# Seven operand blocks with a signal each, a new order of GpSimd's work, and the first rows of the second half beside the last jobs of the first

## The chip, the cores and the metric

One NeuronCore of a Trainium2 chip. The metric is the time of one execution on the device, in microseconds (us). The engines are TensorE (PE; PEld is its weight load), VectorE (DVE), ScalarE (ACT), GpSimd (POOL) and SyncE (SP, which only issues DMAs here). SBUF is the on-chip memory, PSUM the banks that TensorE writes.

## What is computed

A trunk layer over 2048 latent tokens of width 1024 and 256 context tokens. What matters here is its beginning:

```python
h = rmsnorm(x, norm_w) * (1.0 + scale[:, None]) + shift[:, None]
hc = rmsnorm(ctx, norm_w) * (1.0 + scale_c) + shift_c
cols = in_projection(h, w_in, ALL_IN_NAMES)           # h @ w_in, 1024 -> 9 x 1024 + 32
cols_c = in_projection(hc, w_in, ("m_xbc", "m_dt"))
```

Some columns then pass a convolution of width 3 over the tokens (m_xbc with a SiLU behind it, h_proj without), some a SiLU or a sigmoid. The state-space mixer, the long convolutions and the merge come later and are not touched.

## The kernel before

**Products.** The product h @ w_in is made in fp32 quality from parts that TensorE reads fast: each operand is split into a high part (a rounded copy, by ScalarE) and a low part (operand minus high part), and each product is high x high + high x low + low x high: three matmuls. Besides, a pair of weight tiles (128 output channels each) times four blocks of the operand goes with seven block products instead of eight, by sums of blocks on both sides.

**Operand (class Operands).** The tokens go in two halves of 1024. A round k (of KQ = 4) loads two tiles of rows (`load`), multiplies them by the norm (`scale`, DVE) and adds the shift (`shift`, ScalarE), makes T1, T3, T2, N4 (`sums`, GpSimd), then high parts (`high`, ScalarE) and low parts (`low`, DVE) of all seven blocks B11, B21, B22, T1, T2, T3, N4. Before, they went in three groups with a signal each: B11, then B21 with B22, then the four sums in one instruction of 2048 columns. The first half is made in `phase_norm`, beside the projection of the context; the second in `phase_in_projection`, before job NJ. It overwrites the same hi and lo tiles.

**Jobs (phase_in_projection).** A job J is a pair of weight tiles over one half of the tokens, seven products j = 0 to 6 of 12 matmuls each (4 rounds by 3). There are NJ = 37 jobs per half, 74 in all, one of each half with a single tile (J = 8, 45). Jobs 0 to 7 are conv_silu (the first six turned: their rows are also transposed on TensorE and stored by token), 9 to 20 conv, 21 to 36 silu or sigmoid; the second half repeats them from 37 on. Products need the blocks of the weights in the order A11, A12, S2, S3, S1, A22, S4, those of the operand in the order B11, B21, T2, T3, T1, N4, B22.

**The order around a job, written out by hand.** While TensorE makes the products of job J:
- ScalarE, per product j: waits for it, copies product 0 to r1 (L808), makes the high part of block j of job J+1 (`split`, L743; that of S2, S3, S1, S4 waits for its sum), then at j = 3 and 5 `finish` for job J-1 (SiLU or copy, and a store); for turned jobs, at j = 2 and 4, three DMA issues (L773 to L775; two, L777 and L778, in the second half).
- GpSimd: the four sums of the weight tiles of job J+1 (L666 to L671), then its seven low parts (L678).
- DVE: adds each product to the result (`take`, L843 to L859), and between them the convolution of job J-1 (L872 to L885) and the copies of turned rows (L895).
- TensorE: from product 4 on also transposes of job J-1 (L697), behind the signal of `finish`.
- SP: loads weight tiles into three buffers, a tile when the one three before it has been split. The loads for the second half stand in job NJ+1's place.
At job NJ each engine runs all four rounds of the operand, and TensorE waits before each round of each product (L714: the signal of the block's group). raw (two buffers) takes the results of a job and, at the switch, the loaded rows; the sums of the operand lay in res.

## Time and profile before

| | us |
|---|---|
| median of 3 runs | 3819.22 (3813.38 to 3819.71) |
| profiled execution | 3822.45 |
| its span, first to last instruction | 3820.7 |
| TensorE busy | 3432.2 (90%) |
| DVE busy | 2280.6 (60%) |
| GpSimd busy | 1865.3 (49%) |
| ScalarE busy | 1523.4 (40%) |
| mean granted clock of TensorE | 0.950 |

Times of rows are counted from the first instruction. In a group of instructions, the number behind the bar is the busy time, then the mean of one in ns, then the idle time before them and what ended it.

### The profile page before, as it was taken

How to read it: one execution, taken by the hardware profiler on the slowest of the kernel's cores; microseconds unless marked ns; L12 is line 12 of the kernel's file. 1: busy time of each engine (PE TensorE's matmuls, PEld its weight loads, DVE VectorE, ACT ScalarE, POOL GpSimd, SP SyncE). 2: the span in 40 equal slices, each digit the busy share in tenths (PEclk: the TensorE clock that was granted, in tenths of full speed). 3: DMA queues.
4: the chain of work that ended last, by engine and by line, in shares of the span. 5: the costliest groups of instructions: out<-in, count | busy, mean ns of one | idle time of the engine just before them, and what ended most of it. 6: DMA issues, size and time to landing. Idle time of an engine off the chain costs nothing. (4 is left out here: it accounts for less than half of the span.)

```text
span 3820.7 us, 45518 instructions
## 1 busy us (share of the span) xinstructions
PE 3432.2 (90%) x16246; PEld 2839.7 (74%) x16246; DVE 2280.6 (60%) x2870; ACT 1523.4 (40%) x2933; POOL 1865.3 (49%) x1146
## 2 busy tenths in 40 slices
PE   6799999995999999966998999999667886999998
PEld 2677888884888888844996887887546776788886
DVE  5686885224878852236543676666386666577662
ACT  3423223334332233322775554554245553333332
POOL 0477998775879987721000101101167562545442
PEclk8899999997999999988999999999698998999999
DMA  7444333333333333358997847865494445556562
GB/s 260 153 135 142 118 112 107 111 111 109 122 127 116 111 111 111 110 216 330 284 297 197 186 125 166 191 154 120 156 381 157 145 153 167 189 191 212 183 199 99
DMA packets 406346, 636.42 MB, mean 167 GB/s; under 512 B 154731, under 2 KB 241691, under 8 KB 403091
## 3 DMA queue, kind: packets, MB, share of 16 engines
q1 hardware_dynamic: 305661, 442.22, 37.8%
q10 hardware_dynamic: 91256, 157.83, 11.3%
q0 software_dynamic: 9216, 33.56, 3.9%
q8 instruction: 130, 2.13, 0.2%
q14 instruction: 83, 0.68, 0.1%
HBM read 430.49 MB, written 203.03 MB: 166 GB/s over the span
## 5 line engine op out<-in xcount | busy, mean ns | idle before, releaser
L715 PE MATMUL pl_bank<-hl_hi,pl_a_hi 128*128 128x512 f32 x2056 | 811.1, 394 | 67.5 <-DVE hl_lo L354 45.7
L717 PE MATMUL pl_bank<-hl_hi,pl_a_lo 128*128 128x512 f32 x2056 | 803.6, 391 | 0.0
L716 PE MATMUL pl_bank<-hl_lo,pl_a_hi 128*128 128x512 f32 x2056 | 803.0, 391 | 0.0
L715 PEld LDWEIGHTS pl_bank<-hl_hi,pl_a_hi 128*128 128x128 f32 x2056 | 388.0, 189 | 150.5 <-DVE hl_lo L354 37.9
L678 POOL TENSOR_TENSOR pl_a_lo<-pl_sums,pl_a_hi 128x512 fp32r<-128x512 f32 x288 | 433.4, 1516 | 130.1 <-ACT pl_a_hi L743 130.1
L717 PEld LDWEIGHTS pl_bank<-hl_hi,pl_a_lo 128*128 128x128 f32 x2056 | 387.7, 189 | 82.0
L716 PEld LDWEIGHTS pl_bank<-hl_lo,pl_a_hi 128*128 128x128 f32 x2056 | 388.3, 189 | 78.2
L743 ACT ACTIVATE pl_a_hi<-pl_sums 128x512 fp32r<-128x512 f32 x288 | 181.9, 633 | 511.7 <-PE pl_bank L717 468.7
L2018 POOL TENSOR_TENSOR mo_w_lo<-mo_w,mo_w_hi 128x1024 fp32r<-128x1024 f32 x96 | 238.8, 2491 | 276.0 <-ACT mo_w_hi L2089 276.0
L678 POOL TENSOR_TENSOR pl_a_lo<-pl_w,pl_a_hi 128x512 fp32r<-128x512 f32 x220 | 307.7, 1413 | 101.5 <-ACT pl_a_hi L743 101.2
L2046 PE MATMUL mo_bank<-mo_hi,mo_w_hi 128*128 128x512 f32 x768 | 305.9, 398 | 21.4 <-POOL mo_w_lo L2018 17.1
L885 DVE SCALAR_TENSOR_TENSOR pl_res<-pl_raw,pl_taps,pl_res 128x1023 f32<-128x1023 f32 (+1 forms) x160 | 309.4, 1934 | 3.0
L2047 PE MATMUL mo_bank<-mo_lo,mo_w_hi 128*128 128x512 f32 x768 | 300.6, 391 | 0.0
L2048 PE MATMUL mo_bank<-mo_hi,mo_w_lo 128*128 128x512 f32 x768 | 300.4, 391 | 0.0
L1393 DVE TENSOR_TENSOR conv_prod<-conv_bank,conv_spec 128x512 f32<-128x512 f32 x256 | 173.8, 690 | 158.5 <-PE conv_bank L1286 113.3
L743 ACT ACTIVATE pl_a_hi<-pl_w 128x512 fp32r<-128x512 f32 x220 | 137.9, 629 | 290.4 <-PE pl_bank L717 282.5
L1346 ACT COPY conv_v<-conv_bank 128x256 f32<-128x256 f32 x256 | 154.2, 602 | 223.3 <-PE conv_bank L1297 223.3
L1205 POOL DMA_DIRECT2D conv_gin<-u_s x32 | 36.8, 1152 | 382.8 <-DVE conv_x L1358 382.8
L1198 POOL DMA_DIRECT2D conv_x<-u_s x16 | 18.6, 1165 | 385.5 <-POOLq L67 265.9
L2046 PEld LDWEIGHTS mo_bank<-mo_hi,mo_w_hi 128*128 128x128 f32 x768 | 145.0, 189 | 56.8 <-issue 18.4
L1111 DVE COPY spec_y<-spec_bank 64x256 f32<-64x256 f32 x256 | 109.5, 428 | 120.6 <-PE spec_bank L1085 118.6
L843 DVE TENSOR_TENSOR pl_raw<-pl_bank,pl_r 128x512 f32<-128x512 f32 x72 | 49.8, 692 | 207.8 <-PE pl_bank L717 181.6
(247 smaller groups left out, 7093.1 us busy)
## 6 DMA issues: line engine op xcount, KB each, us to landing
pl_w<-in_w_rec SPq DMA_DIRECT2D x146, 512.0 KB, 3.6
conv_spec<-spec_s SPq DMA_DIRECT2D x248, 256.0 KB, 6.1
mo_w<-in_w_br SPq DMA_DIRECT2D x96, 512.0 KB, 3.6
kern_s<-taps_res SPq DMA_DIRECT2D x16, 2048.0 KB, 7.0
spec_xin<-kern_s SPq DMA_DIRECT2D x64, 512.0 KB, 5.4
spec_s<-spec_res ACTq DMA_DIRECT2D x128, 256.0 KB, 4.0
st_xb<-tok_s SPq DMA_DIRECT2D x36, 768.0 KB, 6.4
g_s<-pl_res ACTq DMA_DIRECT2D x32, 512.0 KB, 3.0
```

The costliest lines, as they stand in the source:

```text
L678: nc.gpsimd.tensor_tensor(a_lo[:, n % NS, :], s, a_hi[:, n % NS, :].bitcast(F32), ALU.subtract).then_inc(s_lo, 1)
L715: pe.matmul(out, a_hi[:, q, m], op_hi[:, b, k, :], start=(i == 0 and k == 0), stop=False)
L716: pe.matmul(out, a_hi[:, q, m], op_lo[:, b, k, :], start=False, stop=False)
L717: mm = pe.matmul(out, a_lo[:, q, m], op_hi[:, b, k, :], start=False, stop=(i == len(terms) - 1 and k == KQ - 1))
L743: nc.scalar.activation(a_hi[:, n % NS, :], src, ACT.Copy).then_inc(s_hi, 1)
L885: nc.vector.scalar_tensor_tensor(out=dst, in0=src[:, i:i + width], scalar=taps[i], in1=dst, op0=ALU.mult, op1=ALU.add).then_inc(s_conv, 1)
L1346: nc.scalar.copy(v[:, :, k], bank[2 + k % 2][:, 0:CB]).then_inc(s_vm, 1)
L1393: nc.vector.tensor_tensor(prod[:, n % 4], bank[ubank[k % 4]][:, None, 0:CB].to_broadcast([P, 2, CB]), spec[:, n // 2 % SLOT, :, k % 2], AL ...
L2018: nc.gpsimd.tensor_tensor(w_lo[:, s % 3, :], w[:, s % 3, :], w_hi[:, s % 3, :].bitcast(F32), ALU.subtract).then_inc(s_wlo, 1)
L2046: pe.matmul(bank[s % 4][:], w_hi[:, q, m], hi[:, slot, k, :], start=(k == 0), stop=False)
L2047: pe.matmul(bank[s % 4][:], w_hi[:, q, m], lo[:, slot, k, :], start=False, stop=False)
L2048: mm = pe.matmul(bank[s % 4][:], w_lo[:, q, m], hi[:, slot, k, :], start=False, stop=(k == KT - 1))
```

## The change

- The seven blocks of a round get a signal each, in the order of use (ORDER); `high` and `low` make one block of 512 columns at a time. In `phase_norm` they are spread over three steps. `sums` waits for each block to be free, not for all.
- At the switch the sums of the operand lie in tok, the buffer of turned rows, and no longer in res.
- Round 0 of the second half moves beside job 36 (NJ-1): `scale` after product 3, `shift` after 4, high parts after 5 and 6 and the last two at the head of job 37, before the finishes of job 36; GpSimd's sums of round 0 stand between the low parts of S3 and S1 of job 37. Rounds 1 to 3 stay at the head of job 37. SP waits for DVE's last add of job 36 besides.
- GpSimd makes the low parts of A11 and A12 of a job before the four sums, the other five after them; it waits for the second weight tile only before the sums. The first tile of a pair is given free after the low part of A22.
- The finishes of silu, sigmoid and single jobs move from products 3 and 5 to 0 and 1.

```diff
@@ -289,8 +289,10 @@
     B11, B21, B22, T1, T2, T3, N4 = range(7)
-    GROUP = (0, 1, 1, 2, 2, 2, 2)
-    PARTS = 3
+    ORDER = (B11, B21, T2, T3, T1, N4, B22)
+    PLACE = {b: i for i, b in enumerate(ORDER)}
+    SUM = {T1: 1, T3: 2, T2: 3, N4: 4}
+    PARTS = 7
...
@@ -321,36 +323,50 @@
     def sums(self, pool, k):
...
-        t1, t2, t3, n4 = (self.tmp[:, i // 2, i % 2] for i in range(4))
+        t1, t2, t3, n4 = (self.tmp(b) for b in (self.T1, self.T2, self.T3, self.N4))
+
+        def free(b):
+            if k:
+                pool.wait_ge(self.s_lo, self.PARTS * (k - 1) + self.PLACE[b] + 1)
+
         pool.wait_ge(self.s_norm, 2 * k + 2)
         if k:
-            pool.wait_ge(self.s_lo, self.PARTS * k)
+            pool.wait_ge(self.s_sum, 4 * k)
+        free(self.T1)
         self.nc.gpsimd.tensor_tensor(t1, b12, b11, ALU.subtract).then_inc(self.s_sum, 1)
+        free(self.T3)
         self.nc.gpsimd.tensor_tensor(t3, b22, b12, ALU.subtract).then_inc(self.s_sum, 1)
+        free(self.T2)
         pool.wait_ge(self.s_sum, 4 * k + 1)
         self.nc.gpsimd.tensor_tensor(t2, b22, t1, ALU.subtract).then_inc(self.s_sum, 1)
+        free(self.N4)
         pool.wait_ge(self.s_sum, 4 * k + 3)
         self.nc.gpsimd.tensor_tensor(n4, b21, t2, ALU.subtract).then_inc(self.s_sum, 1)
...
+    def high(self, act, k, i):
+        op, src, hi, lo = self.part(k, i)
+        if op in self.SUM:
+            act.wait_ge(self.s_sum, 4 * k + self.SUM[op])
+        else:
+            act.wait_ge(self.s_norm, 2 * k + (1 if op == self.B11 else 2))
         self.nc.scalar.activation(hi, src, ACT.Copy).then_inc(self.s_hi, 1)
 
-    def low(self, dve, k, g):
-        src, hi, lo = self.part(k, g)
-        dve.wait_ge(self.s_hi, self.PARTS * k + g + 1)
+    def low(self, dve, k, i):
+        op, src, hi, lo = self.part(k, i)
+        dve.wait_ge(self.s_hi, self.PARTS * k + i + 1)
         self.nc.vector.tensor_tensor(lo, src, hi.bitcast(F32), ALU.subtract).then_inc(self.s_lo, 1)
...
@@ -454,11 +470,8 @@
                     k = n // 4
                     if n % 4 == 0:
                         ops.shift(act, k)
-                    elif n % 4 == 1:
-                        ops.high(act, k, 0)
-                        ops.high(act, k, 1)
-                    elif n % 4 == 2:
-                        ops.high(act, k, 2)
+                    for i in ((), (0, 1), (2, 3, 4), (5, 6))[n % 4]:
+                        ops.high(act, k, i)
...
@@ -496,14 +509,15 @@
             for n in range(2 * KT):
                 k = n // 4
                 if n % 4 == 0:
+                    for i in (5, 6) if k else ():
+                        ops.low(dve, k - 1, i)
                     ops.scale(dve, k)
...
+                for i in ((), (), (0, 1), (2, 3, 4))[n % 4]:
+                    ops.low(dve, k, i)
...
+            for i in (5, 6):
+                ops.low(dve, KQ - 1, i)
             conv(2 * KT - 1)
@@ -562,7 +576,7 @@
                 freed[p0[J] + j] = ("act", ea0[J] + 1) if j == 0 else ("dve", ed0[J] + (0, 1, 2, 3, 5, 6, 7)[j])
         w_done[w0[J]] = a0[J] + 2
         if prods is PAIR:
-            w_done[w0[J] + 1] = a0[J] + 6
+            w_done[w0[J]] = w_done[w0[J] + 1] = a0[J] + 6
...
@@ -587,7 +601,7 @@
         s_turn, s_tev, s_tst = ph.sem("turn"), ph.sem("turn_out"), ph.sems("tst", 2)
         ops = Operands(nc, ph, t, keep, rows[:].rearrange("p a n -> p (a n)"), 1, op_hi, op_lo,
                        lambda q, r: raw[:, (NJ + q) % 2, r, 0:HW],
-                       res[:, 0:2, 0:HW].rearrange("p a (b n) -> p a b n", b=2))
+                       lambda b: tok[:].rearrange("p a c n -> p (a c n)")[:, (b - B.T1) * QW:(b - B.T1 + 1) * QW])
@@ -639,6 +653,7 @@
                     sp.wait_ge(s_fin, fin0[NJ - 1])
                     ops.load(sp, 0)
                     sp.wait_ge(s_fin, fin0[NJ])
+                    sp.wait_ge(s_ed, ed0[NJ])
                     for k in range(1, KQ):
                         ops.load(sp, k)
@@ -657,30 +672,42 @@
         def _(pool):
             for J, job in enumerate(jobs):
                 wt = [w[:, (w0[J] + i) % NW, :] for i in range(len(job.tiles))]
-                for i in range(len(job.tiles)):
-                    pool.wait_ge(s_w[(w0[J] + i) % NW], 16 * ((w0[J] + i) // NW + 1))
+                pool.wait_ge(s_w[w0[J] % NW], 16 * (w0[J] // NW + 1))
                 if J:
                     pool.wait_ge(s_lo, a0[J])
+                half = [[tl[:, 0:QW], tl[:, QW:D]] for tl in wt]
+                n = 4 * pairs[J]
+
+                def total(i, x, y, op):
+                    nc.gpsimd.tensor_tensor(sums[:, i], x, y, op).then_inc(s_sum, 1)
+
+                def low(i, src):
+                    at = a0[J] + i
+                    pool.wait_ge(s_hi, at + 1)
+                    nc.gpsimd.tensor_tensor(a_lo[:, at % NS, :], src, a_hi[:, at % NS, :].bitcast(F32), ALU.subtract
+                                            ).then_inc(s_lo, 1)
+
+                low(A11, half[0][0])
+                low(A12, half[0][1])
                 if len(job.tiles) == 2:
-                    n = 4 * pairs[J]
-                    nc.gpsimd.tensor_tensor(sums[:, 0], wt[1][:, 0:QW], wt[1][:, QW:D], ALU.add).then_inc(s_sum, 1)
+                    pool.wait_ge(s_w[(w0[J] + 1) % NW], 16 * ((w0[J] + 1) // NW + 1))
+                    total(0, half[1][0], half[1][1], ALU.add)
                     pool.wait_ge(s_sum, n + 1)
-                    nc.gpsimd.tensor_tensor(sums[:, 1], sums[:, 0], wt[0][:, 0:QW], ALU.subtract).then_inc(s_sum, 1)
-                    nc.gpsimd.tensor_tensor(sums[:, 2], wt[0][:, 0:QW], wt[1][:, 0:QW], ALU.subtract).then_inc(s_sum, 1)
+                    total(1, sums[:, 0], half[0][0], ALU.subtract)
+                    total(2, half[0][0], half[1][0], ALU.subtract)
                     pool.wait_ge(s_sum, n + 2)
-                    nc.gpsimd.tensor_tensor(sums[:, 3], wt[0][:, QW:D], sums[:, 1], ALU.subtract).then_inc(s_sum, 1)
-                    src = (wt[0][:, 0:QW], wt[0][:, QW:D], sums[:, 1], sums[:, 2], sums[:, 0], wt[1][:, QW:D], sums[:, 3])
-                else:
-                    src = (wt[0][:, 0:QW], wt[0][:, QW:D])
-                for i, s in enumerate(src):
-                    n = a0[J] + i
-                    pool.wait_ge(s_hi, n + 1)
-                    nc.gpsimd.tensor_tensor(a_lo[:, n % NS, :], s, a_hi[:, n % NS, :].bitcast(F32), ALU.subtract
-                                            ).then_inc(s_lo, 1)
+                    total(3, half[0][1], sums[:, 1], ALU.subtract)
+                    low(S2, sums[:, 1])
+                    low(S3, sums[:, 2])
+                    if J == NJ:
+                        for q in range(2):
+                            pool.wait_ge(s_tst[q], 16 * stores_before(t0[NJ] + q))
+                        ops.sums(pool, 0)
+                    low(S1, sums[:, 0])
+                    low(A22, half[1][1])
+                    low(S4, sums[:, 3])
                 if J == NJ:
-                    for q in range(3):
-                        pool.wait_ge(s_st[q], 16 * ((f0[NJ] + 2 - q) // 3))
-                    for k in range(KQ):
+                    for k in range(1, KQ):
                         ops.sums(pool, k)
@@ -710,7 +737,7 @@
                         q = (a0[J] + a) % NS
                         for k in range(KQ):
                             if J == NJ:
-                                pe.wait_ge(ops.s_lo, B.PARTS * k + B.GROUP[b] + 1)
+                                pe.wait_ge(ops.s_lo, B.PARTS * k + B.PLACE[b] + 1)
...
@@ -782,16 +809,19 @@
             for J, prods in enumerate(products):
                 nxt = a0[J + 2] - a0[J + 1] if J + 1 < 2 * NJ else 0
                 if J == NJ:
+                    act.wait_ge(s_mm, p0[NJ])
+                    ops.high(act, 0, 5)
+                    ops.high(act, 0, 6)
                     for m in order(J - 1):
                         finish(J - 1, m)
-                    act.wait_ge(s_mm, p0[NJ])
-                    ops.shift(act, 0)
-                    for k in range(KQ):
+                    ops.shift(act, 1)
+                    for k in range(1, KQ):
                         ops.high(act, k, 0)
                         ops.high(act, k, 1)
                         if k + 1 < KQ:
                             ops.shift(act, k + 1)
-                        ops.high(act, k, 2)
+                        for i in range(2, B.PARTS):
+                            ops.high(act, k, i)
                 for j in range(max(len(prods), nxt, 7)):
                     if j < len(prods):
                         n = p0[J] + j
@@ -808,10 +838,15 @@
                             nc.scalar.activation(r1[:], bank[n % 4][:], ACT.Copy).then_inc(s_ea, 1)
                     if j < nxt:
                         split(J + 1, j)
-                    if J and J != NJ and j in (3, 5):
-                        m = (j == 3) * 1
-                        if m in order(J - 1):
-                            finish(J - 1, m)
+                    if J and J != NJ:
+                        for m in order(J - 1):
+                            if j == (5 - 2 * m if jobs[J - 1].conv is not None else 1 - m):
+                                finish(J - 1, m)
+                    if J == NJ - 1:
+                        if j == 4:
+                            ops.shift(act, 0)
+                        for i in {5: (0, 1, 2, 3), 6: (4,)}.get(j, ()):
+                            ops.high(act, 0, i)
                     if j == 2 and J >= 2 and jobs[J - 2].turned:
@@ -905,20 +940,27 @@
             when = {0: ((1, 0), (1, 1)), 1: ((1, 2),), 2: ((0, 0),), 3: ((0, 1), (0, 2))}
             for J, prods in enumerate(products):
                 if J == NJ:
-                    dve.wait_ge(s_mm, p0[NJ])
-                    ops.scale(dve, 0)
-                    for k in range(KQ):
+                    for i in (4, 5, 6):
+                        ops.low(dve, 0, i)
+                    ops.scale(dve, 1)
+                    for k in range(1, KQ):
                         ops.low(dve, k, 0)
                         ops.low(dve, k, 1)
                         if k + 1 < KQ:
                             ops.scale(dve, k + 1)
-                        ops.low(dve, k, 2)
+                        for i in range(2, B.PARTS):
+                            ops.low(dve, k, i)
                 for j in range(7):
                     if prods is PAIR:
                         take(J, j)
                     if J and jobs[J - 1].conv is not None:
                         for m, op in when.get(j, ()):
                             conv(J - 1, m, op)
+                    if J == NJ - 1:
+                        if j == 3:
+                            ops.scale(dve, 0)
+                        for i in (0, 1, 2, 3) if j == 6 else ():
+                            ops.low(dve, 0, i)
                     if j < len(prods) and turn_at(J, j):
                         turned_out(*turn_at(J, j))
```

## Rows read from the trace of the kernel before

**Rows 1.** Page, costliest groups: one of TensorE's three of the in-projection
```profile
L715 PE MATMUL pl_bank<-hl_hi,pl_a_hi 128*128 128x512 f32 x2056 | 811.1, 394 | 67.5 <-DVE hl_lo L354 45.7
```
**Rows 2.** Waits of PE, 160 to 1665 us: total us, times, longest
```profile
PE pl_bank L715 <- DVE hl_lo L354: 45.7, 5, 11.9
...
PE pl_turned L697 <- ACT pl_res L753: 6.4, 6, 2.2
```
**Rows 3.** Timeline (start, length, what, [idle before]), a conv job: ACT, POOL
```profile
500.65 0.60 ACT L808 ACTIVATE pl_r<-pl_bank 128x512 f32<-128x512 f32 x1 [2.00 <-PE pl_bank L717]
...
519.69 0.60 ACT L808 ACTIVATE pl_r<-pl_bank 128x512 f32<-128x512 f32 x1 [2.01 <-PE pl_bank L717]
...
517.76 1.30 POOL L678 TENSOR_TENSOR pl_a_lo<-pl_sums,pl_a_hi 128x512 fp32r<-128x512 f32 x1 [0.40 <-ACT pl_a_hi L743]
```
**Rows 4.** Timeline, start of the in-projection: ACT, POOL, PE
```profile
165.47 1.15 ACT L743 ACTIVATE pl_a_hi<-pl_w 128x512 fp32r<-128x512 f32 x2 [7.88 <-DMA pl_w<-in_w_rec]
...
171.88 2.49 POOL L678 TENSOR_TENSOR pl_a_lo<-pl_w,pl_a_hi 128x512 fp32r<-128x512 f32 x2
...
173.29 0.77 PE L715 MATMUL pl_bank<-hl_hi,pl_a_hi 128*128 128x512 f32 x1 [21.78 <-POOL pl_a_lo L678]
```
**Rows 5.** Timeline, DVE: a long and a short low part of the operand
```profile
119.77 2.28 DVE L354 TENSOR_TENSOR hl_lo<-nl_tmp,hl_hi 128x2048 fp32r<-128x2048 f32 x1
...
907.31 0.69 DVE L354 TENSOR_TENSOR hl_lo<-pl_raw,hl_hi 128x512 fp32r<-128x512 f32 x1 [1.73 <-ACT hl_hi L349]
```
**Rows 6.** Timeline, ACT: r1 copies of jobs 36 and 38
```profile
881.45 0.60 ACT L808 ACTIVATE pl_r<-pl_bank 128x512 f32<-128x512 f32 x1 [2.01 <-PE pl_bank L717]
...
971.43 0.60 ACT L808 ACTIVATE pl_r<-pl_bank 128x512 f32<-128x512 f32 x1 [2.01 <-PE pl_bank L717]
```
**Rows 7.** The switch: timeline of ACT and DVE; DMA issues (KB, median us to landing)
```profile
900.07 1.06 ACT L763 ACTIVATE pl_res<-pl_raw 128x1024 f32<-128x1024 f32 x1 [0.46 <-ACT pl_res L763]
...
903.10 2.47 DVE L311 SCALAR_TENSOR_TENSOR pl_raw<-pl_raw,keep_mod,rt_rows 128x1024 f32<-128x1024 f32 x2 [4.64 <-DMA pl_raw<-in_xT]
...
924.11 2.47 DVE L311 SCALAR_TENSOR_TENSOR pl_raw<-pl_raw,keep_mod,rt_rows 128x1024 f32<-128x1024 f32 x2 [2.61 <-DMA pl_raw<-in_xT]
...
pl_raw<-in_xT SPq DMA_DIRECT2D x8, 512.0 KB, 5.2
```
**Rows 8.** Job 4: timeline of ACT, DVE, PE; L885's ns min/median/max
```profile
268.72 0.63 ACT L743 ACTIVATE pl_a_hi<-pl_w 128x512 fp32r<-128x512 f32 x1 [2.15 <-PE pl_bank L717]
271.93 0.64 ACT L743 ACTIVATE pl_a_hi<-pl_sums 128x512 fp32r<-128x512 f32 x1 [2.58 <-PE pl_bank L717]
...
277.11 1.04 ACT L753 ACTIVATE pl_res<-pl_res 128x1023 f32<-128x1023 f32 x1
...
269.25 2.09 DVE L885 SCALAR_TENSOR_TENSOR pl_res<-pl_raw,pl_taps,pl_res 128x1023 f32<-128x1023 f32 x1
...
278.20 0.66 PE L697 MATMUL pl_turned<-pl_ident,pl_res 128*128 128x128 f32 x4 [0.70 <-ACT pl_res L753]
...
L885 DVE SCALAR_TENSOR_TENSOR pl_res<-pl_raw,pl_taps,pl_res x160: 1275/2194/2332, 196.0 to 1371.7; 128x1023 f32<-128x1023 f32 x80, 128x1025 f32<-128x1025 f32 x80
```
**Rows 9.** Job 2: ACT, PE; stretches (us, busy of each engine, PEclk, DMA, GB/s)
```profile
225.05 4.73 ACTq L775 DMA_DIRECT2D tok_s<-pl_tok  x1
...
231.53 1.08 PE L697 MATMUL pl_turned<-pl_ident,pl_res 128*128 128x128 f32 x4 [2.15 <-ACT pl_res L753]
...
232.84 0.63 PE L716 MATMUL pl_bank<-hl_lo,pl_a_hi 128*128 128x512 f32 x1
...
232.00:234.00 2.00, 2.00 (x7) 1.71 (x7) 0.00 (x0) 0.61 (x1) 1.28 (x1) 0.50 0.83 293
...
910.00:920.00 10.00, 0.67 (x2) 0.57 (x3) 5.58 (x5) 5.67 (x5) 5.51 (x5) 0.50 0.02 4
```
**Rows 10.** Timeline, ACT: job 41
```profile
1037.94 0.64 ACT L743 ACTIVATE pl_a_hi<-pl_w 128x512 fp32r<-128x512 f32 x1 [2.16 <-PE pl_bank L717]
...
1044.01 0.64 ACT L743 ACTIVATE pl_a_hi<-pl_sums 128x512 fp32r<-128x512 f32 x1 [2.23 <-PE pl_bank L717]
```

30 lines of the change are left out of this document (12 added, 18 removed).

## Prediction

> **What bounds the kernel now.** I read the page first: TensorE is busy for 90% of the span, and its three largest groups (one of them is [rows 1]), some 800 us each, are the in-projection. So only what stops TensorE there counts. The view of its waits over that stage lists 45.7 us in five waits for DVE's low parts of the operand and 6.4 us in six waits for ScalarE's finished rows [rows 2]; a third, of 21.8 us for GpSimd's low part of the weights, is the start [rows 4]. In a plain job the engine is full: from one r1 copy to the next is 19.04 us, seven products of 2.72 [rows 3]. Shorter work on another engine gains nothing there, and a later step costs nothing until its slack is used up. What the two stalls at the starts can give back is known; the question is what the new order of GpSimd and ScalarE does to the jobs between them.
>
> **1. First job of the in-projection.** GpSimd now makes the low part of A11 before the four sums. Before, the high part of A11 was ready at 166.05 (165.47 and half of the 1.15 us for two), the low part came out at 173.1, and TensorE began at 173.29 [rows 4]. Now the low part takes 1.25 us from 166.1, so TensorE begins at 167.5: 5.8 us earlier. The third product needs low S2, behind low A12 and four sums: seven operations of 1.25 to 1.27 from 166.1 end near 175.0, while two products (4.55 and 2.72, the first at the low clock) end at 174.8. It gives back 0.4. **-5.4 us** (-4 to -6).
>
> **2. Context stage (phase_norm).** DVE's groups follow each other without idle time there, so DVE sets the pace. Three low subtractions per pair of rows become seven of 512 columns. One of 2048 took 2.28 us, one of 512 0.69 [rows 5]. Four short ones for a long one cost between nothing (the extra time is overlap at their ends) and 4 x 0.69 - 2.28 = 0.48; I take 0.25 in each of four rounds: **+1.0 us** (0 to 2; the four sums beside them contend as before).
>
> **3. The switch to the second half.** The r1 copies before and after lie at 881.45 and 971.43, 90.0 us for two jobs that need 38.1 [rows 6]: 51.9 us is the most that could go. The clock is at its lower level (0.50) in this stretch [rows 9]. Today the first rows are scaled at 903.10, behind the finishes of job 35, and each later round ends with the low parts of the sums, then a load (5.2 us to landing, its pair 0.2 to 0.4 behind: 5.4), for which DVE waits before it scales, as at 924.11 [rows 7].
> The change moves round 0 beside the last pair of jobs. Job 35's two finishes move to the first two products of job 36, so rows 0 are asked for at 885.9 (881.45, and the r1, A11 and A12 copies and the finish that now follow) and land near 892, beside two stores. Scaling (2.5) and shifting (1.2 more) end at 895.7, the four sums at 901. But the next rows overwrite the buffer of job 36 and so wait for both of its finishes, and these now stand behind all seven high parts of round 0 on ScalarE: B22's ends at 902.9, the finishes (1.06 and 0.46 before it, each) at 905.5 where the second ended at 901.1. So the load of round 1 is 4.4 us later than now. It lands at 912; scale and shift to 915.6; the two low parts beside GpSimd to 919.4; scale 2 and its shift to 923; five high parts and the last low parts, two of them beside GpSimd, to 927.5; load of round 3 to 933; scale and shift to 936.5; five high parts and B11 to 939.7; low B11 of round 3 near 941.7. From there TensorE never waits again, since each block has its own signal: the end of product 0 at the low clock (1.3), product 1 partly so (3.8), five of 2.72: 960.5. Today that job ends at 968.5. **-8.0 us** (-3 if one more low part is held up in each round, -14 if the loads land in 4.5 us and no low part is). So 44 of the 51.9 us stay.
> The rule "2.0 us + bytes / 436 GB/s" of the Trainium skill (DMA: Bandwidth & Descriptors, "Anatomy of one DMA") makes 4.4 us of a pair of loads, where the rows show 5.4; with two on the chain the whole sum would be 2 us less by it. I go by the rows.
>
> **4. Turned jobs, first half (2 to 6).** This is where the change takes back. ScalarE's copy of S2 waits for sums 0 and 1. Before, GpSimd had them done while ScalarE waited for TensorE; now they stand behind low A12, which waits for A12's high part, which waits for product 1. In job 4 [rows 8]: A12's copy ends at 269.35. DVE's scalar_tensor_tensor gets the port at 269.25 and, alone, takes 1.28: GpSimd waits to 270.5 (today it is DVE that waits there: 2.09 us). Low A12 to 271.8, sum 0 to 273.0, sum 1 to 274.3. S2's copy starts there instead of 271.93: 2.4 us later (1.4 with no contention; 3.1 if the next DVE operation gets in too). Behind it on ScalarE stand the three DMA issues of the turned rows (some 4.5 us whatever the start: the third one alone took 4.73 in job 2, where no store of turned rows was under way before [rows 9]), S3's copy, the SiLU at 277.11, and for that SiLU TensorE waits already: its transposes start at 278.20, just after it ends at 278.15. So all of the delay reaches TensorE, and so every job of the five gets longer: 5 x 2.4 = 12.1 us. Job 1 has no such issues; its S3 copy comes 1.8 later, of which 0.9 shows.
> The port rule of the Trainium skill (SBUF — State Buffer, "SBUF: two separate sides") says that whoever starts first holds the shared pair for the whole instruction. By it each held GpSimd operation takes its full 1.29 after the release; the rows give about 1.15. The copy would be 0.1 later per job, 0.7 us in the sum.
> **The clock.** In job 2 TensorE stood still for 2.15 us before the transposes, and the granted clock fell to 0.50 between 232 and 235; matmuls took 0.63 instead of 0.39 us and about 1.3 us was lost [rows 9]. In the other jobs it idles less (0.70 in job 4, 4.2 us over five of them by [rows 2]) and the clock stays. With 2.4 more, jobs 3 to 6 idle 3.1 to 3.5, longer than what let it fall. I add 4 x 1.3 = 5.2. Sum of part 4: **+18.2 us** (+8 with 1.4 and no fall, +25 with 3.1 and falls in all six).
>
> **5. Turned jobs, second half (38 to 43).** Fewer descriptors, so no long issue, and TensorE does not wait today. S3's copy now waits for sum 2: A12's copy ends at 1038.58, low A12 at 1040.9, sum 1 at 1043.5, DVE's tensor_scalar 0.55, sum 2 at 1045.2; the copy starts there instead of at 1044.01 [rows 10]. The SiLU ends at 1046.9, product 4 ended near 1046.5: 0.4 us in each of five jobs. In job 38, the first SiLU after the sigmoids, a table load stands between S3's copy and the SiLU, and TensorE waits for it already; it comes 1.95 us later in full, and the wait grows to some 2.8 us, so I add 1.3 for the clock. **+5.2 us** (+1 to +9).
>
> **6. The plain and conv jobs, moved finishes, loads.** GpSimd is busy 18.5 of 19.04 us in a conv job (its longest wait there is 0.40) [rows 3], and the new order makes it idle 1.8 us before A11 and 1 before A12. It does not become the bound: DVE's operations now run in these gaps instead of against it, and S4's low part ends about 1 us later than now, while low A11 cannot start before the high one anyway. Its product is 14 us away, S2's 7. The second weight tile is now loaded after low A22, not low A12, and so some 10 us later; it lands about 4 us before sum 0 wants it. SP's queue has the context loads behind it, which are needed a job later. The finishes of silu and sigmoid jobs move from products 3 and 5 to 0 and 1, where ScalarE waits 1.7 us for TensorE. Nothing.
>
> **Sum.** -5.4 + 1.0 - 8.0 + 18.2 + 5.2 = +11.0 us. The profiled execution took 3822.45 us (3820.7 of span and 1.75 around it), so 3833.4 by it; it lies 3.2 above the median 3819.22, so I say **3830.2**.
>
> **Rivals.**
> A, the forecast: 3830, by its own bounds 3827 to 3838. Chance 0.50.
> B, the same mechanism, small: the clock does not fall and the copy is 2 us late: 11.0 - 6.5 - 2 = +2.5, 3822. For it: idle of 1 us left the clock alone. 0.22.
> C, the switch gives its upper bound, -14: +5, 3824. 0.08.
> D, faster. The third DMA issue ends when the queue has drained, at a time of its own, and not a fixed time after its start; then S3's copy and the SiLU come as today and part 4 is 0.9. With the switch at -10: -5.4 + 1 - 10 + 0.9 + 5.2 = -8.3, 3811. It decides once the SiLU of jobs 2 to 6 is under 0.8 us late. Against it: the issue is longest in job 2, with an empty queue. 0.10.
> E, GpSimd becomes the bound in the 28 conv jobs: if DVE's operations don't fit the gaps, each job leaves it 0.6 us later, and after some ten the slack of S2 is gone; another 12 us, 3842. 0.10.
> Under 0.2% (7.6 us) a measurement of this kernel tells little from no change. Slower by more: A nearly whole, E: 0.59. Same: B, C, the lower edge of A: 0.31. Faster: 0.10. The range reaches from below B and C, 3814 (part 4 at its lower bound of 8 with the rest as forecast gives 3820, the switch at -14 with it 3814), to E, 3841.
>
> **What would show it.** In the trace after: TensorE's first in-projection matmul some 5 us after the first weight lands; S2's copy in jobs 2 to 6 about 9 us after the r1 copy (6.5 now) and r1 copies over 25 us apart (22.7 now); clock 0.50 once in each; r1 copies 82 us apart across the switch, the load of round 1 near 905; low parts of plain jobs on time. It would be wrong if the copy of S2 were late and the SiLU not, or if r1 copies of conv jobs were over 19.04 apart.

## The result, and the profile of the changed kernel

| | before | changed |
|---|---|---|
| median of 10 runs each, us | 3818.99 | 3839.24 |
| lowest to highest | 3813.38 to 3821.63 | 3826.02 to 3845.56 |
| profiled execution, us (its span) | 3822.45 (3820.7) | 3835.30 (3833.5) |
| mean granted clock in it | 0.950 | 0.951 |

The ratio of the medians' runs is 1.005, 95% interval 1.0041 to 1.0059: slower by about 19 us, or 20 by the medians. One execution of all those told of below took 5129 us, at a mean granted clock of 0.644; no ratio includes it. The forecast was 3830.2, with 3841 as its upper end. The direction is right, the size is 9 us short, and the way there is right only in part.

Page and waits of the changed kernel, as in [rows 1] and [rows 2] (same stretch, 160 to 1665 us; L742 is the old L715, L724 the old L697, L770 the old L743, L687 the old L678):

```profile
L742 PE MATMUL pl_bank<-hl_hi,pl_a_hi 128*128 128x512 f32 x2056 | 813.1, 395 | 64.3 <-DVE hl_lo L370 41.8
...
PE pl_bank L742 <- DVE hl_lo L370: 41.8, 4, 16.6
PE pl_bank L742 <- POOL pl_a_lo L687: 22.5, 4, 15.4
PE pl_turned L724 <- ACT pl_res L780: 18.5, 12, 4.6
```

The operand's wait fell by only 4 us, and that for finished rows grew from 6.4 to 18.5. Inside the 22.5 us for GpSimd are two waits of 3.3 in the middle of the stage that were not there before. The start, as [rows 4] (columns: start, length, engine, line, what, [idle before it <- released by]):

```profile
165.33 1.15 ACT L770 ACTIVATE pl_a_hi<-pl_w 128x512 fp32r<-128x512 f32 x2 [7.98 <-DMA pl_w<-in_w_rec]
...
166.10 2.49 POOL L687 TENSOR_TENSOR pl_a_lo<-pl_w,pl_a_hi 128x512 fp32r<-128x512 f32 x2 [17.47 <-ACT pl_a_hi L770]
...
167.51 0.76 PE L742 MATMUL pl_bank<-hl_hi,pl_a_hi 128*128 128x512 f32 x1 [15.44 <-POOL pl_a_lo L687]
```

TensorE begins at 167.51 where it began at 173.29. To see where this goes, I took the first matmul of every job from PE's timeline in both traces, and call the time to the next job's first matmul the job's length:

| job | before | changed | difference | forecast |
|---|---|---|---|---|
| start of job 0 | 173.29 | 167.51 | -5.8 | -5.8, and +1.0 for the context stage |
| 0 | 20.87 | 21.22 | +0.4 | +0.4 |
| 1 | 20.14 | 26.91 | +6.8 | +0.9 |
| 2, 3, 4 | 25.43, 22.70, 22.36 | 23.65, 23.70, 23.24 | -1.8, +1.0, +0.9 | +2.4, +3.7, +3.7 |
| 5, 6 | 22.72, 22.73 | 23.45, 25.75 | +0.7, +3.0 | +3.7, +3.7 |
| 9 and 46 (each follows the single-tile job) | 19.28, 19.29 | 24.44, 24.43 | +5.2, +5.1 | 0 |
| 36 and 37 (switch) | 89.98 | 84.74 | -5.2 | -8.0 |
| 38 | 20.68 | 24.10 | +3.4 | +3.25 |
| 39 to 43, each | 21.2 | 21.8 | +0.56 | +0.4 |
| plain and conv jobs | 19.04 | 19.04 | 0 | 0 |

The sum is +16.5 us at the start of the last job. The spans differ by 12.8: stages in which nothing was changed took 3.7 less in this one execution, and in the medians the difference is 20.

**Job 4**, as [rows 8]:

```profile
269.32 0.63 ACT L770 ACTIVATE pl_a_hi<-pl_w 128x512 fp32r<-128x512 f32 x1 [2.15 <-PE pl_bank L744]
274.97 0.63 ACT L770 ACTIVATE pl_a_hi<-pl_sums 128x512 fp32r<-128x512 f32 x1 [5.01 <-POOL pl_sums L682]
...
276.16 1.75 ACTq L802 DMA_DIRECT2D tok_s<-pl_tok  x1
278.03 0.63 ACT L770 ACTIVATE pl_a_hi<-pl_sums 128x512 fp32r<-128x512 f32 x1 [2.43 <-issue]
278.57 1.04 ACT L780 ACTIVATE pl_res<-pl_res 128x1023 f32<-128x1023 f32 x1
...
279.66 0.65 PE L724 MATMUL pl_turned<-pl_ident,pl_res 128*128 128x128 f32 x4 [1.56 <-ACT pl_res L780]
```

S2's copy comes 5.65 us after A12's where it was 3.2: 2.4 late, as worked out, and GpSimd's sums are named. But the third store issue behind it takes 1.75 us where it took 3.57, and the SiLU is only 0.9 late against the r1 copy. In jobs 3, 5 and 6 it is 1.0, 0.7 and 1.4 late, in job 2 not at all.

**Job 9**, which no step of the prediction looked at:

```profile
370.10 0.62 ACT L770 ACTIVATE pl_a_hi<-pl_w 128x512 fp32r<-128x512 f32 x1
...
370.80 1.28 POOL L687 TENSOR_TENSOR pl_a_lo<-pl_w,pl_a_hi 128x512 fp32r<-128x512 f32 x1 [5.82 <-ACT pl_a_hi L770]
372.04 1.28 POOL L682 TENSOR_TENSOR pl_sums<-pl_w 128x512 f32<-128x512 f32 x1
...
374.72 0.63 ACT L770 ACTIVATE pl_a_hi<-pl_sums 128x512 fp32r<-128x512 f32 x1 [4.00 <-POOL pl_sums L682]
...
378.51 0.71 PE L742 MATMUL pl_bank<-hl_hi,pl_a_hi 128*128 128x512 f32 x1 [3.29 <-POOL pl_a_lo L687]
```

The single-tile job has two long products (5.44 and 8.16 us). A12's high part waits for the second, so its low part waits too, and GpSimd stands idle for 5.82 us with the four sums behind that wait. Job 9's third product needs low S2, and TensorE stands 3.3 us for it. The kernel before has the same wait of 5.82 us, but it had made the sums ahead of both low parts (job 8 starts at 350.61 there, job 9 at 364.21):

```profile
343.99 2.29 POOL L671 TENSOR_TENSOR pl_sums<-pl_w,pl_sums 128x512 f32<-128x512 f32 x1
357.49 2.29 POOL L678 TENSOR_TENSOR pl_a_lo<-pl_w,pl_a_hi 128x512 fp32r<-128x512 f32 x1 [11.21 <-ACT pl_a_hi L743]
365.60 1.30 POOL L678 TENSOR_TENSOR pl_a_lo<-pl_w,pl_a_hi 128x512 fp32r<-128x512 f32 x1 [5.82 <-ACT pl_a_hi L743]
```

**Job 1**, and the clock (in the last three lines: stretch and its length; busy time of PE, PEld, DVE, ACT, POOL; granted clock; DMA's busy share and GB/s):

```profile
207.11 1.12 PE L724 MATMUL pl_turned<-pl_ident,pl_res 128*128 128x128 f32 x4 [4.61 <-ACT pl_res L780]
...
205.00:207.00 2.00, 0.00 (x0) 0.00 (x0) 0.46 (x1) 1.52 (x2) 2.00 (x3) 0.50 0.00 0
232.00:234.00 2.00, 1.26 (x8) 1.13 (x9) 1.73 (x3) 1.32 (x2) 2.00 (x2) 1.00 0.53 162
...
379.00:381.00 2.00, 2.00 (x6) 1.59 (x5) 0.00 (x0) 1.54 (x3) 2.00 (x3) 0.50 0.37 149
```

After job 9's stall the granted clock is at its lower level, 0.50 (1.2 GHz), as it was in job 2 before [rows 9]; in job 2 of the changed kernel it is 1.00. Outside the switch it fell in jobs 1, 6, 9, 38 and 46, each time in or just behind a pause of 2.3 us or more.

### The profile page after: what moved, and what is told of

The parts are those of the page before. It is cut to its first block and busy times, and to the rows that moved or that the text cites. A ratio compares the mean times of both kernels' runs of the same rounds, so it can differ in the third digit from the quotient of the medians.

```text
span 3833.5 us, 45593 instructions
## 1 busy us (share of the span) xinstructions
PE 3439.1 (90%) x16246; PEld 2840.7 (74%) x16246; DVE 2268.1 (59%) x2902; ACT 1525.3 (40%) x2965; POOL 1846.5 (48%) x1146
## 5 line engine op out<-in xcount | busy, mean ns | idle before, releaser
L742 PE MATMUL pl_bank<-hl_hi,pl_a_hi 128*128 128x512 f32 x2056 | 813.1, 395 | 64.3 <-DVE hl_lo L370 41.8
L743 PE MATMUL pl_bank<-hl_lo,pl_a_hi 128*128 128x512 f32 x2056 | 804.9, 391 | 0.0
L742 PEld LDWEIGHTS pl_bank<-hl_hi,pl_a_hi 128*128 128x128 f32 x2056 | 389.1, 189 | 148.4 <-DVE hl_lo L370 41.4
L687 POOL TENSOR_TENSOR pl_a_lo<-pl_w,pl_a_hi 128x512 fp32r<-128x512 f32 x220 | 339.3, 1544 | 243.3 <-ACT pl_a_hi L770 241.9
L743 PEld LDWEIGHTS pl_bank<-hl_lo,pl_a_hi 128*128 128x128 f32 x2056 | 389.3, 189 | 78.8
L687 POOL TENSOR_TENSOR pl_a_lo<-pl_sums,pl_a_hi 128x512 fp32r<-128x512 f32 x288 | 412.5, 1453 | 54.5 <-ACT pl_a_hi L770 54.5
L770 ACT ACTIVATE pl_a_hi<-pl_sums 128x512 fp32r<-128x512 f32 x288 | 181.7, 633 | 569.1 <-POOL pl_sums L682 372.3
L2088 PE MATMUL mo_bank<-mo_hi,mo_w_hi 128*128 128x512 f32 x768 | 306.0, 398 | 23.3 <-POOL mo_w_lo L2060 17.1
L920 DVE SCALAR_TENSOR_TENSOR pl_res<-pl_raw,pl_taps,pl_res 128x1023 f32<-128x1023 f32 (+1 forms) x160 | 277.8, 1736 | 3.0
L770 ACT ACTIVATE pl_a_hi<-pl_w 128x512 fp32r<-128x512 f32 x220 | 137.9, 629 | 253.8 <-PE pl_bank L744 225.2
L682 POOL TENSOR_TENSOR pl_sums<-pl_w 128x512 f32<-128x512 f32 x144 | 203.7, 1414 | 0.7 <-DMA pl_w<-in_w_rec 0.6
```

What stands on the lines that cost most here:

```text
L682: nc.gpsimd.tensor_tensor(sums[:, i], x, y, op).then_inc(s_sum, 1)
L687: nc.gpsimd.tensor_tensor(a_lo[:, at % NS, :], src, a_hi[:, at % NS, :].bitcast(F32), ALU.subtract).then_inc(s_lo, 1)
L742: pe.matmul(out, a_hi[:, q, m], op_hi[:, b, k, :], start=(i == 0 and k == 0), stop=False)
L743: pe.matmul(out, a_hi[:, q, m], op_lo[:, b, k, :], start=False, stop=False)
L770: nc.scalar.activation(a_hi[:, n % NS, :], src, ACT.Copy).then_inc(s_hi, 1)
L920: nc.vector.scalar_tensor_tensor(out=dst, in0=src[:, i:i + width], scalar=taps[i], in1=dst, op0=ALU.mult, op1=ALU.add).then_inc(s_conv, 1)
```

## The experiments

All ran beside the kernel before; its median in these comparisons was 3816 to 3819 us.

### Two ends: the order of the sums alone, and all but it

The first is the kernel before, with only this changed: GpSimd's order (told in words here) and, since the sums need it, the later release of the first tile (`w_done` counts the low parts after which a tile is given free):

```
-                totals 0 to 3; low A11, A12, S2, S3, S1, A22, S4
+                low A11, A12; totals 0 to 3; low S2, S3, S1, A22, S4
-        w_done[w0[J]] = a0[J] + 2
+        w_done[w0[J]] = a0[J] + 6
```

> The kernel before, with GpSimd's new order and the later release of the first weight tile alone; nothing of the switch, the seven blocks or the finishes is changed. Theory 1 (order of the sums): TensorE starts 5 us earlier, job 1 takes 26.9 us, jobs 9 and 46 take 24.4, job 38 some 24, jobs 39 to 43 some 21.8; the switch is as before. From the differences of the two traces 3819 + 21 = 3840 us. Theory 3 (moved finishes): jobs 9 and 46 stay at 19.3 and the time is near 3830. The prediction's own terms give 3819 + 18 = 3837, with job 1 at 21 and jobs 2 to 6 at 26.

3835.1 us, ratio 1.004 (1.0026 to 1.0053). Jobs 9 and 46 take 24.3 and 24.4 us, job 1 24.9, jobs 2 to 6 23.5, 25.5, 23.2, 24.8 and 23.9; the switch is as before (89.5). The second is the changed kernel with the old order, and the old release of the first tile, back from job 1 on (in short):

```
+                ahead = J == 0 or len(job.tiles) == 1
+                if ahead: low(A11), low(A12)
                 total 0 to 3
+                if not ahead: low(A11), low(A12)
                 low(S2) ...
```

> The changed kernel, with GpSimd's old order (four sums, then low A11 and A12) and the old release of the first weight tile in every job but the first. The first job keeps the new order; the seven blocks, the rows of round 0 beside the last pair, and the moved finishes stay. Theory 1 (the sums standing behind low A12 make the stalls): jobs 9 and 46 fall from 24.4 us to 19.3, jobs 2 to 6 go back to 22.4 to 25.4, jobs 39 to 43 to 21.2, job 38 to 20.7; the switch keeps its -5. Of the 5.8 us that the first job gives, most is lost in job 1 anyhow, since GpSimd works without a pause from 166 us to the end of job 1 in both kernels and ends there only 0.8 us earlier: about 3813 us. Theory 2 (the prediction's: the gain of the start stays): 3808. Theory 3 (the moved finishes or the later loads make the stalls of jobs 9 and 46): these stay at 24.4 if it is the finishes, about 3823.

3809.4 us, ratio 0.9977 (0.9966 to 0.9987), which is faster than the kernel before by 0.2%. Jobs 9 and 46 are back at 19.3, jobs 2 to 6 at 23.8, 22.7, 22.3, 22.6 and 22.7, jobs 39 to 43 at 21.2. Beside job 9's start ScalarE now finds the sums made, and takes two without a wait:

```profile
361.43 1.14 ACT L777 ACTIVATE pl_a_hi<-pl_sums 128x512 fp32r<-128x512 f32 x2
...
361.61 1.30 POOL L689 TENSOR_TENSOR pl_a_lo<-pl_w,pl_a_hi 128x512 fp32r<-128x512 f32 x1 [5.82 <-ACT pl_a_hi L777]
362.87 3.80 POOL L689 TENSOR_TENSOR pl_a_lo<-pl_sums,pl_a_hi 128x512 fp32r<-128x512 f32 x3
```

GpSimd still waits 5.82 us, with nothing behind it that is wanted. So the order costs what the change loses, and the moved finishes, which both this kernel and the changed one have, are not the cause in jobs 9 and 46.

### Which low part does it

The changed kernel with low A11, the sums, then low A12, from job 1 on, and the old release of the first tile there.

> The changed kernel, with GpSimd's order low A11, four sums, low A12 from the second job on, and the old release of the first weight tile. Theory 1 in its narrow form: only low A12 in front of the sums hurts, since its high part waits for the second product of the job before; low A11 needs only the r1 copy. Then S2's copy starts 9.5 us after the job's first matmul as before, jobs 9 and 46 take 19.3 us, and the time is that of the run with the sums first, about 3813, give or take 2. In its wide form (any low part in front of the sums hurts): S2's copy is about 1 us late, job 9 and 46 some 1 us, jobs 2 to 6 some 0.5 us each, 3818.

3813.5 us, ratio 0.9988 (0.9979 to 0.9997). Jobs 9 and 46 take 19.3, jobs 39 to 43 21.2: low A12 in front of the sums is what hurts there. In jobs 1 and 2 to 6 it is not wholly free: 25.9; 25.4, 22.7, 23.3, 22.6, 25.7, with clock falls in jobs 1, 2 and 6. The profiled execution took 3826.7 us, the longest of its 11, so these lengths may be on the high side; the kernel before has 25.4 in job 2 as well. What of the rest is the order's is open.

### The later load

The changed kernel, where the first tile of a pair is released after low S2 (`a0[J] + 3`) instead of low A22.

> The changed kernel with one thing undone in half: the first weight tile of a pair is given back after low S2, the first low part that comes after all four sums, and no longer after low A22. Theory 1 (the later loads play no part): all jobs as in the changed kernel, job 1 at 26 to 27 us, jobs 9 and 46 at 24.4, the time within 3 us of it (3839). Theory 4 (the second weight tile lands late and holds the sums): job 1 is 2 us or more shorter, and sum 0 of job 2 starts before 198 us.

3837.3 us; job 1 27.1, jobs 9 and 46 24.4, sum 0 of job 2 at 199.34 us (199.23 in the changed kernel). In the changed kernel the later load of the first tile's buffer plays no part.

### What the first job's early start is worth

The same kernel as the second above, with the old order in job 0 too.

> The run with the sums first, but in the first job too, so that nothing of GpSimd's order is new; the seven blocks, round 0 beside the last pair, and the moved finishes stay. Against the run with the sums first in all jobs but the first (3809) it prices the new order of the first job alone. Theory 1 (GpSimd is the chain from the first weights to the end of job 1, so that most of the earlier start is given back): TensorE starts 5.8 us later, jobs 0 and 1 together are 3 to 4.5 us shorter, 1.5 to 2 us in all: 3811. Prediction's theory (0.4 given back): 5 us, 3814. The switch should be 85 us for its two jobs in both.

3813.0 us, ratio 0.9981 (0.9972 to 0.9990), so all of the change but GpSimd's order is worth some 7 us (4 to 11 by the interval). TensorE starts at 173.63; jobs 0 and 1 take 20.8 and 20.1, where the kernel with the early start needs 22.0 and 22.9 after 167.28. Of 6.3 us, 3.9 are given back (1.2 in job 0, 2.7 in job 1) and 2.4 stay, about as expected. The medians can't tell: they differ by 3.6, the ratios to the kernel before by 0.0004, which is 1.5 us. GpSimd shows one reason. In the kernel before it works from 166.87 to 193.7 us without a pause of over 0.25, and has a little slack from there; in the changed one it works from 166.10 to 210.3 with one pause of 0.5. TensorE began 5.8 us earlier, its supplier 0.8.

In the kernel with the sums first there is a second reason, which no run takes apart from the first. Before the first sum of job 1 GpSimd stands still for a weight tile (issued at 178.48, landed at 181.74), whose buffer the first job gives free only after low A22:

```profile
182.25 1.28 POOL L684 TENSOR_TENSOR pl_sums<-pl_w 128x512 f32<-128x512 f32 x1 [2.55 <-DMA pl_w<-in_w_rec]
```

Without that wait the sum would start at 179.7, 12.4 us behind TensorE's first matmul and not 15.0. That is an estimate; in the next kernel it starts 12.2 behind, and there job 1 takes 20.3. So most of what job 1 gives back here may be the load's. In the changed kernel, where two low parts stand ahead of the sums, the tile landed at 182.59, just before the sum at 182.93, and the earlier release above gained nothing.

### Taking GpSimd off that chain

On the kernel with the sums first and stores issued earlier (next section), DVE makes the seven low parts of job 0, and GpSimd only its sums; the first tile is given free after the last of them:

```
+            for i in (A11, A12, S2, S3, S1, A22, S4):      # DVE, before its first job
+                dve.wait_ge(s_hi, i + 1)
+                nc.vector.tensor_tensor(a_lo[:, i, :], first[i], a_hi[:, i, :].bitcast(F32), ALU.subtract).then_inc(s_lo, 1)
```

> The run with the turned stores issued one product earlier (3808), with one thing more: DVE, which is idle there, makes all seven low parts of the first job (0.69 us each where GpSimd takes 1.26), and GpSimd only the four sums. Theory 1 (GpSimd's chain from 166 us gives back the early start in job 1): TensorE starts at 166.9, GpSimd reaches the sums of job 1 some 5 us earlier, the pause of some 2.8 us in job 1 and its clock fall go (25.0 to some 20.2), job 0 needs 21: 5 to 6 us less, 3802. Rival: the pause in job 1 comes from ScalarE's own order behind the product, then job 1 stays at 23 to 25 and the time is 3808.

3798.2 us, ratio 0.9945 (0.9931 to 0.9958). Jobs 0 and 1 take 20.8 and 20.3, where the kernel without this edit takes 22.3 and 25.0. Two things moved at once: GpSimd has seven operations less, and the weight tile is asked for at 175.49 instead of 178.17, since DVE's low parts end sooner. GpSimd had stood 3.33 us for that tile. An earlier release with the low parts left on GpSimd was not tried, so the share of each is open.

Then the same together with the edit at the switch, told below:

> The run with the finishes first at the switch (3801) and the one with DVE making the first job's low parts (3798), together. The two edits touch different stretches, 166 to 208 us and 865 to 950 us; both were measured on the same base of 3808. If they add up: the switch's two jobs take 80.8 us and not 85.8, jobs 0 and 1 take 41.1 and not 45.3, 3793 to 3794 us. If the later start of the first job was only moved into something that follows (as the start in job 1 was), the sum stays above 3797.

3795.1 us (3789.9 to 3801.4): 3 below the run before, where 4.8 were expected, and 6 below the edit at the switch alone. In its profiled execution, the longest of the five, job 1 takes 24.7 again. The first sum of job 1 on GpSimd, here first in the run without, then in the run with the switch's edit:

```profile
179.37 1.30 POOL L684 TENSOR_TENSOR pl_sums<-pl_w 128x512 f32<-128x512 f32 x1 [6.26 <-DMA pl_w<-in_w_rec]
```

```profile
181.34 1.28 POOL L684 TENSOR_TENSOR pl_sums<-pl_w 128x512 f32<-128x512 f32 x1 [7.86 <-DMA pl_w<-in_w_rec]
```

The load was issued at 175.5 and 175.9 and landed at 179.2 and 181.2. With GpSimd out of the way the weights' load is next, and its landing varies. So it was asked for earlier:

```
                     if n == NW:
+                        sp.wait_ge(s_lo, 2); sp.wait_ge(s_sum, 4)
```

> All the edits together (3795), with one thing more: the first tile of the first pair is given back once the four sums and its own two low parts are done (173.5 us), and no longer after the last low part of the first job (175.5 us). In the profiled execution of all edits together the load behind it landed at 181.2 us, GpSimd started the sums of job 1 at 181.3, and job 1 took 24.7 us; in the run without the edit at the switch it landed at 179.2 and job 1 took 20.3. If the landing of this load decides (theory 1), it lands at 177 to 179, GpSimd starts 2 us earlier, and job 1 takes 20.1 to 20.4 us in every execution: 3791 to 3794. If GpSimd's start has nothing to do with it, 3795 and job 1 still between 20 and 25.

3793.7 us (3789.4 to 3794.8), ratio 0.993 (0.9916 to 0.9944). This execution reached the stage 2 us earlier (first matmul at 165.20), so I count from there: the sum starts 9.4 us behind it, where it was 12.2 and 13.8, and job 1 takes 20.14, its length in the kernel before:

```profile
174.59 1.28 POOL L687 TENSOR_TENSOR pl_sums<-pl_w 128x512 f32<-128x512 f32 x1 [3.50 <-DMA pl_w<-in_w_rec]
```

That it is so in every execution can't be told from one profile. This is the kernel with the lowest median of the study, 23 us under the kernel before; its ratio's interval overlaps those of the two kernels ahead (0.9931 to 0.9958, 0.9924 to 0.9951).

### The long store issue

Where the third issue ends decides what a late S2 costs, and it was rival D. Edit: `if j == 2 and J >= 2` becomes `if j == 1 and J >= 2`, on the kernel with the sums first, and then on the kernel before.

> The run with the sums first, with one thing more: ScalarE issues the first three stores of turned rows in the gap after its second copy instead of after the third. If the long third issue takes a fixed time after its start (3.6 to 4.7 us), it ends 3 us earlier, the SiLU comes when DVE has its rows ready, and the pauses of TensorE in jobs 2 to 6 (1.1 to 2.5 us before their transposes) go: 5 to 8 us faster than the run with the sums first. If the issue ends when its queue has drained, at a time of its own, the SiLU starts at 15 us of the job as now and nothing is gained. The traces so far lie between: an issue that starts 2.5 us later ends 0.9 later.

> The kernel before, with one thing changed: the first three stores of turned rows are issued one product earlier. It prices TensorE's pauses in the turned jobs of the first half alone, without anything of the change. From the trace of the run that had this edit on another base: jobs 2 to 6 take 21.5 us each and not 25.4, 22.7, 22.4, 22.7, 22.7, 8.6 us less: 3819 - 8.6 = 3810. If DVE's later steps give some back, 3814.

3807.6 us (3809.4 without; the intervals of the two overlap) and 3814.2 (ratio 0.9989, 0.9979 to 0.9999). In both, jobs 2 to 6 take 21.5 us each in the profiled execution, 6.7 and 8.6 less than without it, and TensorE no longer waits before the transposes:

```profile
264.42 2.07 ACTq L809 DMA_DIRECT2D tok_s<-pl_tok  x1
...
272.13 0.60 PE L731 MATMUL pl_turned<-pl_ident,pl_res 128*128 128x128 f32 x4
```

The third issue starts 7.2 us into job 4 and takes 2.07; in the kernel before it starts at 10.5 and takes 3.57, in the changed one at 13.2 and takes 1.75. Over jobs 2 to 6 the three are 2.1 to 2.5, 3.6 to 4.7 and 1.8 to 3.0. It has neither a fixed length nor a fixed end (9.3, 14.0 and 14.9 us into the job). Beside the one of 3.57 runs a weight load that was issued at 272.4 and landed at 279.7; beside the other two runs hardly any (one landed at 276.4, 0.3 us after the issue began; one was issued at 267.2, after its end). That this is why it is long was not tried. Of the 6.7 us gained on the kernel with the sums first its median shows 1.8; job 1, whose code is the same, took 25.0 us in this execution and 22.9 in the other. Of the 8.6 us gained in jobs 2 to 6 the median of the last kernel shows about 2 to 4: its first matmul came 1.5 and its switch 1.4 us later in the profiled execution, and the rest is open.

### The switch

On the kernel with both edits (sums first, stores earlier), the two finishes of job 36 go ahead of the five last high parts of round 0 (a part is left out):

```
-                    for m in order(J - 1):
-                        finish(J - 1, m)
...
+                        if j == 6:
+                            for m in order(J): finish(J, m)
-                        for i in {5: (0, 1, 2, 3), 6: (4,)}.get(j, ()):
+                        for i in {5: (0, 1), 6: (2, 3, 4)}.get(j, ()):
```

> The run with the turned stores issued one product earlier (3808), with the two finishes of the last job of the first half ahead of the high parts of T2, T3, T1, N4 and B22 of round 0, and no longer behind them. If the load of round 1 behind these finishes is what sets the rest of the switch, as the prediction's chain says, it is issued 4 us earlier; of this 2.6 us reach round 1's scaling (DVE's low parts of round 0 end later instead), and the two jobs take 83 instead of 85.6 us: 3805. If the low parts on DVE beside GpSimd's sums set it alone, nothing changes.

3801.0 us (3807.6 without), ratio to before 0.995 (0.9936 to 0.9963, where it was 0.9952 to 0.998 without). Jobs 36 and 37 take 80.8 us instead of 85.6, so 4.8 and not 2.6. SP's loads of rounds 1 to 3, without and with the edit (job 36 starts at 869.86 and 867.32):

```profile
897.31 23.52 SPq L307 DMA_DIRECT2D pl_raw<-in_xT  x6
```

```profile
889.95 23.51 SPq L307 DMA_DIRECT2D pl_raw<-in_xT  x6
```

The first is issued 27.5 and 22.6 us into job 36: the whole of the difference is in that one load, which stood behind the high parts.

### The clock

In the changed kernel, ahead of the wait for the first SiLU of each turned job:

```
+                    for _ in range(9):
+                        pe.matmul(turned[n % 2][:], op_hi[:, 0, 0, 0:P], op_hi[:, 0, 0, :], start=True, stop=True)
```

> The changed kernel (3839), with nine matmuls of 512 columns added ahead of each wait for the first SiLU of a turned job (jobs 1 to 6 and 38 to 43); their result is overwritten by the transposes and is used by nothing. They take about 9 x 0.23 = 2.0 us, less than the pauses of 1.9 to 5.0 us in jobs 1 to 6 and 2.75 in job 38, and 1.3 more than the 0.7 of jobs 39 to 43, which so get 6 us longer in all. If the granted clock falls because TensorE stands still (theory 1), it stays at 1.00 in jobs 1 to 6 and 38 apart from what the start leaves, and each fall avoided saves 1.2 to 1.5 us: three such falls in the profiled execution (jobs 1, 6, 38), more in other executions. Net: 3839 - 4 + 6 = 3841, with jobs 2 to 6 all at 23.2 to 23.9 and job 38 at 22.8. If the falls come at times of their own, they stay: 3845.

3840.6 us. Job 6, with the clock behind the pause:

```profile
322.83 2.21 PE L722 MATMUL pl_turned<-hl_hi 128*128 128x512 f32 x9
324.88 0.60 PE L727 MATMUL pl_turned<-pl_ident,pl_res 128*128 128x128 f32 x4
...
325.00:327.00 2.00, 2.00 (x13) 1.70 (x12) 1.01 (x2) 0.63 (x1) 2.00 (x2) 1.00 0.76 277
```

Jobs 2 to 6 take 23.5 us each (job 6: 25.75 without), job 1 25.0 (26.9), job 38 22.6 (24.1). The clock does not fall in one of them. Of the two jobs of the same 3.29 us pause that have no filler, 46 keeps its fall, but 9 has none in this execution (22.8 us, 24.4 in the changed kernel); and in job 1 a pause of 2.59 us is left behind the filler, without a fall. Jobs 39 to 43 pay 1.5 us each. So the filler fits a clock that falls because TensorE stands still, but one execution, with a pause of 3.29 us that let nothing fall, does not show it. By these three jobs, one execution against another, a fall costs 1.5 to 2.3 us, the forecast's 1.3 or more. That other executions of the changed kernel have more falls than the profiled one, which would make up its distance of 4 us from the median, remains a guess: this run's median is no lower.

## Why the prediction was right in direction and short in size

- **First job.** TensorE's start is 5.8 us earlier, 0.25 of it from the stage ahead, and job 0 gives back 0.35: right to 0.3 us. The step that failed is the end of the account there. I looked whether job 0 could use the start, and not whether GpSimd was ahead in job 1. It makes eleven operations of 1.26 to 1.3 us per job from 166 us on with hardly a pause; job 1 took 26.9, +6.8 where I had +0.9. With the old order from job 1 on, job 1 takes 22.9, so 4.0 of it go with the order, and they hold the late S2 and whatever the clock's fall costs; the 2.7 that are left go with the early start, by GpSimd's chain or by the weight tile, which is open. This rests on one execution of each kernel: with that same code job 1 took 22.9, 25.0 and 23.3 us.
- **Context stage.** +1.0 forecast; the in-projection's first DMA is issued at 160.47 instead of 160.72, so -0.25, below the lower end of 0 that I gave. From kernel to kernel that issue lies between 158.8 and 160.9 us with the new blocks and between 159.7 and 162.0 with the old, so no run shows the term, and none shows that it is nothing to a few tenths.
- **Turned jobs, first half.** The mechanism is right to 0.1 us (S2's copy 2.4 late, behind low A12 and two sums). The term is wrong: +3.8 instead of +17.3. "A third issue of fixed length" was the failed step. It was up to half shorter when later, so that 0.9 of 2.4 us reached the SiLU in job 4, and of jobs 3 to 6, where I had counted a clock fall each, it fell in job 6 alone; job 2 lost its fall. Rival D's price for these five jobs (nothing) was nearer than mine, though its sign, a SiLU under 0.8 us late, holds in jobs 2 and 5 alone. My own signs failed here: one r1 copy over 25 us after the last, not five, and one fall, not five.
- **Second half.** Jobs 39 to 43 +0.56 against 0.4, job 38 +3.4 against 3.25 with its clock fall: right, step by step, where no long issue stands between.
- **"The plain jobs: nothing."** Right for the 19.04 us of plain and conv jobs (rival E is out), and wrong by 10.3 us for jobs 9 and 46. I had reasoned for one kind of predecessor, a pair. After the single-tile job, A12's high part waits 8.16 us for one product. The kernel with the old order, but all else of the change, has both jobs at 19.3.
- **The switch.** -5.2 for -8.0: the term is mis-sized. Up to the load of round 1 the chain holds: issued 23.9 us after the r1 copy of job 36 (24.05 forecast), shift 2 ends at +41.9 (+41.5). Then DVE's low parts beside GpSimd's sums took more than I gave them:

```profile
915.68 0.85 SPq L307 DMA_DIRECT2D pl_raw<-in_xT  x2
...
922.93 2.47 DVE L313 SCALAR_TENSOR_TENSOR pl_raw<-pl_raw,keep_mod,rt_rows 128x1024 f32<-128x1024 f32 x2 [4.53 <-DMA pl_raw<-in_xT]
...
936.69 5.10 DVE L370 TENSOR_TENSOR hl_lo<-pl_raw,hl_hi 128x512 fp32r<-128x512 f32 x3
```

  Three took 5.10 (1.70 each; 0.69 alone [rows 5]) and end at +50.0, not at +46. This comes twice, part of it hidden by the load. It is my own bound "-3 if one more low part is held up in each round", halfway. The pair of loads of round 1 took 7.2 us from first issue to last landing, beside a store and the pair of round 2, and that of round 3 5.8. The Trainium skill's rule (DMA: Bandwidth & Descriptors, "Anatomy of one DMA") gives, as an estimate, 4.4; neither agrees. That section of the Trainium skill makes its fit for DMAs that GpSimd issues, and these are SyncE's.
- **Sum.** The misses partly cancel: -1.0 (start with the context stage), +5.9 (job 1), -13.5 (jobs 2 to 6), +10.3 (jobs 9 and 46), +2.8 (switch), +1.0 (38 to 43) make +5.5; with the forecast's +11.0 that is the +16.5 of the trace. The forecast time is near for a reason that is not its own: that it lies in the range is in part luck. (Rival E's price, 3842, lies 1 us outside the range that was said to reach it.)

## What to carry to other kernels

Before an in-order engine's work is reordered, list for every operation what its predecessor in the new order waits for, once for each kind of neighbouring job: the exception (here one single-tile job in each half) cost 5.2 us each time, the pair jobs 39 to 43 0.56. A start moved forward keeps its gain only if every supplier moves forward with it; look for the engine that has no idle time behind the start, and for the load whose buffer that engine gives free. The new order was needed in one job only, and there DVE was free to do more.

## What the runs showed of the hardware

- The issue of the same kind of store (the third of the turned rows) on ScalarE's queue took from 1.75 to 5.6 us in jobs 2 to 7: 3.6 to 4.7 when it came 10.5 us into a job of the kernel before, 2.1 to 2.5 at 7.2. What makes it long is open.
- TensorE's pauses in jobs 1 to 9 and 38 to 46, over the profiled executions of all kernels but the one with the filler: none of the 25 of 0.5 to 2.1 us went with a lower granted clock, 21 of the 27 longer ones did. With nine useless matmuls in the pauses of jobs 1 to 6 and 38 it stayed at 1.00, in one execution, and there it stayed so behind a bare pause of 3.29 us too.
- A low part on DVE (0.69 us alone) and a sum on GpSimd (1.28 alone) both took 1.7 us in the switch while they ran beside each other, one of each in every 1.7 us, where one behind the other would make 1.97 for the two.
